# Two transformer layers and a mixture-of-experts block on one core: the first two halves of four projections multiplied tile by tile, with a new start and a new mixer order

## What is computed

```python
for l in range(DEPTH):                                   # DEPTH = 2, D_MODEL = 1024
    mod = silu_c @ w_mod[l] + b_mod[l]                   # shifts, scales and gates, six of each
    h = modulate(rms_norm(x, norm1[l]), sh1, sc1)        # and hc from ctx
    na_q, na_k, na_v, gq, gk, gv, ga, gb = split(h @ w_in[l])
    ...                                                  # two attentions
    x = x + g1 * branch_merge(ya, yb, ga, gb, w_pa[l], w_pb[l], w_o[l])
    h2 = modulate(rms_norm(x, norm2[l]), sh2, sc2)
    x = x + g2 * swiglu(h2, w_ffn_in[l], w_ffn_out[l])   # ctx too, in layer 0
x = rms_norm(x, final_norm)
# second block
conv_v, conv_g, lru_x, lru_g = split(rmsnorm(x, g_mix) @ w_in)
y_conv = silu(layernorm(causal_depthwise_conv(conv_v * sigmoid(conv_g), 31 taps)))
xr = causal_depthwise_conv(lru_x, 4 taps)
y_lru = rglru(xr) * gelu(lru_g)                          # gates from xr, a decay, a scan
x = x + concat(y_conv, y_lru) @ w_out
x = x + routed_experts(...); x = x + gate(x) * e
return rmsnorm(x, g_final)
```

## Time and profile before

| what | value |
|---|---|
| time, median of 3 runs | 3089.24 us (3089.12 to 3089.36) |
| the profiled execution's own time | 3086.72 us |
| its span, first to last instruction | 3084.8 us |
| TensorE busy | 2908.3 us, 94% of the span |
| VectorE, ScalarE, GpSimd busy | 958.2, 937.5, 829.0 us |
| mean granted TensorE clock | 0.975 |
| the start, to the first multiplication of x | 52.9 us |
| layer 0 / layer 1 | to about 1302 us / to about 2210 us |
| mixer | about 2210 to 2430 us |
| experts and output | from there |

### The profile page before, as it was taken

The page is one execution under the profiler, slowest core; times in us unless marked ns, Lnnn a source line. Parts: engine busy times, 40 slices in busy tenths (PEclk is TensorE's granted clock), DMA queues, the critical chain, the costliest instruction groups (busy, mean ns, idle before and its releaser), DMA issues.

```text
span 3084.8 us, 40562 instructions
## 1 busy us (share of the span) xinstructions
PE 2908.3 (94%) x16366; PEld 2149.8 (70%) x16366; DVE 958.2 (31%) x1409; ACT 937.5 (30%) x1598; POOL 829.0 (27%) x644
## 2 busy tenths in 40 slices
PE   6999889998999999999988989999989899999998
PEld 4887668887888888868767768888744744444443
DVE  2505550123111111160542122222487323232324
ACT  3226442123221122232643233222464211111131
POOL 3323223334222322443313444444410200000011
PEclk9999999999999999999999989999999899999999
DMA  5124321111111221212421222232220469999940
GB/s 206 55 69 165 110 90 62 61 62 48 62 59 57 69 68 51 79 41 79 155 83 63 88 96 82 84 110 88 87 87 28 198 287 402 409 401 409 401 194 27
DMA packets 62183, 406.48 MB, mean 132 GB/s; under 512 B 7232, under 2 KB 8656, under 8 KB 18160
## 3 DMA queue, kind: packets, MB, share of 16 engines
q1 hardware_dynamic: 57600, 393.77, 34.3%
q0 software_dynamic: 1872, 6.72, 0.6%
q10 hardware_dynamic: 2592, 4.30, 0.4%
HBM read 402.66 MB, written 2.10 MB: 131 GB/s over the span
## 4 chain that ended last, share of the span: by engine, by line
PE 79%; issue 8%; DVE 4%; ACT 4%; POOL 3%; DMA 1%; ACTq 0%; POOLq 0%; DVEq 0%
PE ps L585 45%; PE ps L1026 7%; PE ps L1049 4%; PE ps L753 3%; POOL half_slots L1619 3%; PE ps L780 3%; PE ps L734 3%; PE ps L1068 2%; PE ps L1096 2%; PE ps L992 2%; PE ps L621 2%; PE ps L594 1%; PE ps L913 1%; PE ps L610 1%; DVE expert_parts L2338 1%
## 5 line engine op out<-in xcount | busy, mean ns | idle before, releaser
L585 PE MATMUL ps<-h_parts,half_slots 128*128 128x512 f32 (+1 forms) x5952 | 1164.7, 357 | 38.1 <-POOL half_slots L1619 14.5
L585 PEld LDWEIGHTS ps<-h_parts,half_slots 128*128 128x128 f32 x5952 | 983.8, 190 | 219.0 <-issue 31.2
L1619 POOL TENSOR_TENSOR half_slots<-ring,half_slots 128x1024 fp32r<-128x1024 f32 (+3 forms) x280 | 600.1, 2144 | 1083.6 <-ACT half_slots L1164 1083.2
L1164 ACT ACTIVATE half_slots<-ring 128x1024 fp32r<-128x1024 f32 (+3 forms) x280 | 267.5, 956 | 1271.8 <-PE ps L585 1260.7
L585 PE MATMUL ps<-hidden_parts,half_slots 128*128 128x512 f32 (+1 forms) x1584 | 305.1, 355 | 0.0
L585 PEld LDWEIGHTS ps<-hidden_parts,half_slots 128*128 128x128 f32 x1584 | 261.0, 188 | 43.6
L585 PE MATMUL ps<-y_parts,half_slots 128*128 128x512 f32 (+1 forms) x1152 | 229.3, 359 | 9.9 <-DVE y_parts L1940 9.7
L1026 PE MATMUL ps<-second_block,scratch 128*64 128x512 f32 x1024 | 223.3, 594 | 1.4 <-ACT scratch L1549 0.9
L585 PEld LDWEIGHTS ps<-y_parts,half_slots 128*128 128x128 f32 x1152 | 192.9, 191 | 44.3 <-issue 11.8
L1026 PEld LDWEIGHTS ps<-second_block,scratch 128*64 128x64 f32 x1024 | 74.6, 137 | 142.8 <-issue 142.8
L1993 DVE TENSOR_TENSOR first_block<-ps,first_block 128x768 f32<-128x768 f32 (+1 forms) x44 | 36.3, 825 | 434.0 <-PE ps L585 434.0
(11 more groups left out here) (313 smaller groups left out, 2969.9 us busy)
## 6 DMA issues: line engine op xcount, KB each, us to landing
second_block<-experts SPq DMA_DIRECT2D x192, 1024.0 KB, 9.0
ring<-stream SPq DMA_DIRECT2D x146, 1024.0 KB, 4.8
ring<-stream SPq DMA_DIRECT2D x16, 768.0 KB, 4.2
...
```

What stands on the lines that cost most here:

```text
L585: last = nc.tensor.matmul(ps[s % 2][:, a:b], part(x, s)[:, k, :], parts[y][:, tile + k, a:b], start=start and k == 0 and n == 0, stop=stop ...
L1164: act.activation(part(0, s), raw_half(s), ACT.Copy).then_inc(hi_done, 1)
L1619: nc.gpsimd.tensor_tensor(part(1, s), raw_half(s), part(0, s).bitcast(fp32), ALU.subtract)\
```

## The change

1. *Start.* The eight `mod_head` slots get places of their own (`head_low`, `head_high`, in memory that is not yet used), so all eight transfers, one transfer for x behind the second of them, and the first slots of `gq` are issued at once. TensorE has the copied rows of two slots at a time (`HROW`), turns slot n-1 behind slot n's products, and sums squares and spreads 1/rms between slots (behind slots 4 and 6). The sums of squares are VectorE's, `rstd(0)` as well between its copies.
2. *First pair.* `first_pair` replaces the first two calls of `product` for `gq` and `ffn_in0` in both layers. The third half's parts go to a place outside `half_slots`, and `upper` for it waits one step less.
3. *Mixer.* TensorE: convolution, mean, gates, variance behind half 11. ScalarE and VectorE have the layer norm ahead of the recurrence; VectorE scales half 10 before its last five taps of tile 1. The sums lie in the free halves of banks 0 and 1.

```diff
+HEAD = 8
+def fills(n):
+    return 16 * ((n - HEAD) // RING + 1)
...
+        third = {}
+        for l in range(LAYERS):
+            third[2 * SLOT0[l, "gq"] + 2] = third_gq
+            third[2 * SLOT0[l, "ffn_in0"] + 2] = third_ffn
+
         def part(x, s):
+            if s in third:
+                return view(third[s], x * D, KD, P)
...
             def load(n, i=0):
                 m = n - RING
+                if m < HEAD:
+                    m = -1
...
+            for n in range(HEAD):
+                sp.dma_start(head_slot(n), stream[n]).then_inc(head_in[n // 2], 16)
+                if n == 1:
+                    sp.dma_start(X[:, :, :].rearrange("p k n -> p (k n)"), x_tiles).then_inc(x_loaded, 16)
...
+            def first_pair(s, nt, ready):
+
+                def tile(half, k):
+                    for a, b in pieces(nt):
+                        for n, (x, y) in enumerate(((0, 0), (0, 1), (1, 0))):
+                            last = nc.tensor.matmul(ps[half][:, a:b], part(x, s + half)[:, k, :], HS[y][:, k, a:b],
+                                                    start=k == 0 and n == 0, stop=k == KD - 1 and n == 2)
+                    if k == KD - 1:
+                        last.then_inc(steps, 1)
+
+                wait_half(s)
+                pe.wait_ge(lo_done, splits(s))
+                for k in range(KD + 1):
+                    if k < KD:
+                        ready(k)
+                        tile(0, k)
+                    if k == 1:
+                        wait_half(s + 1)
+                        pe.wait_ge(lo_done, splits(s + 1))
+                    if k:
+                        tile(1, k - 1)
...
-            for n in range(8):
-                mod_slot(n, 2 * n, 0, n == 0)
-            mod_turn()
+            for n in range(HEAD):
+                head_rows(n)
+                if n:
+                    head_turn(n - 1)
+                if n == 4:
+                    sum_squares(0, T)
+                if n == 6:
+                    spread_sum(0, T)
+            head_turn(HEAD - 1)
...
                 if j == 11:
-                    lru_gates()
                     convolve(0)
                     conv_mean()
-                if j == 12:
+                    lru_gates()
                     conv_variance()
...
-            for k in range(KD):
-                act.dma_start(X[:, k, 0:NL], xT[k * P:(k + 1) * P, :]).then_inc(x_loaded, 16)
-                act.dma_start(X[:, k, NL:T], ctxT[k * P:(k + 1) * P, :]).then_inc(x_loaded, 16)
...
-                act.wait_ge(steps, per * i + (s - 1))
+                act.wait_ge(steps, per * i + (s - 2 if s in third else s - 1))
...
+                root(2 * l, T)
                 if l == 0:
                     upper(2 * SLOT0[0, "gq"])
                     upper(2 * SLOT0[0, "gq"] + 1)
-                root(2 * l, T)
...
-            convolve(1, 20, TAPS)
+            convolve(1, 20, 26)
             scale_half(10)
+            convolve(1, 26, TAPS)
             scale_half(11)
             convolve(2, 2, TAPS)
```

161 lines of the change are left out of this document (107 added, 54 removed).

## The result

The changed kernel takes 3063.72 us (median; 3062.45 to 3065.93), the kernel before 3089.18 in the same comparison: a ratio of 0.9921, 95% interval 0.9909 to 0.9933, so 20.7 to 28.1 us less. Measured again later beside other variants it came out at 0.9931 (0.9917 to 0.9944). The forecast was 3068.8 us, 20.4 us less, inside 3060 to 3078. The two profiled executions of the changed kernel have spans of 3061.6 and 3066.3 us, against 3084.8.

The account below looks back on a forecast made before the run. TensorE, busy 94% of the span, was taken as the bound, with time to win only in its waits or half-clock matmuls. Terms 1.7 + 5.4 + 3.8 + 1.0 + 8.5 = 20.4 us gave 3068.8 us from 3089.24, range 3060 to 3078.

Parts of the forecast that it names:

- start: Program start: mod_head slots with own places and x as one transfer bring x's first multiplication to 51.2 us; gain 1.7 us.
- gq and ffn_in0, layer 0: Layer 0's first projection and FFN halves, alternated tile by tile: 2.7 us each (1.8 to 3.5), 5.4 us.
- gq, layer 1: Layer 1's first projection pair: h stays the bound, three tiles follow the last one in place of nine; gain 3.8 us.
- ffn_in0, layer 1: Layer 1's first FFN pair: S + 14.0 against S + 14.8; gain 1.0 us (0 to 2).
- mixer up to w_out2's third half: Second block's mixer, reordered: third half of w_out2 11.5 us earlier, less low-clock deductions; gain 8.5 us, ends 3 and 12.
- Rival 4: Start: x as one transfer needs 8 us at 386 GB/s or slows the kernel; 3089 to 3110, say 3098; chance 0.02.
- Rival 3: Pairs do nothing, alternating costs its gain or half 2 waits: 10 us fall away, 3079; chances 0.05, 0.03 with mixer eaten.
- Four gate products (1.7) run: Mixer, after the mean: four gate products take 1.7 us, then TensorE waits 2.3 us for ScalarE's squares and first sigmoid.
- the deduction for low clock: Mixer: about 1.5 us taken off behind the gates' wait, and 1.5 us behind the wait ahead of w_out2's third half.
- The tail keeps its order: Mixer after half 15: last lower part at 2376.5 (2388.0 before), w_out2's third half at 2386.3 instead of 2397.85.
- Rival 2: Mixer's gain eaten by low clock and ScalarE as bound for halves 14 and 15: 2 to 4 us remain, 3075; chance 0.17.
- Rival 1: Start reaches full clock: x multiplied at about 44 us, 7 us more gain, 3062; chance 0.16.

## Why the prediction was right, step by step

The forecast and its range held, and each term came near the trace, two of them in part by errors that cancelled (in us; the two traces of the changed kernel against the one of before):

| term | forecast | first | again |
|---|---|---|---|
| start | 1.7 | 2.4 | 1.9 |
| gq and ffn_in0, layer 0 | 5.4 | 5.3 | 4.9 |
| gq, layer 1 | 3.8 | 4.1 | 4.1 |
| ffn_in0, layer 1 | 1.0 | 1.8 | 0.6 |
| mixer up to w_out2's third half | 8.5 | 7.7 | 7.8 |
| sum | 20.4 | 21.3 | 19.3 |
| span | | 23.2 | 18.5 |

What lies between sum and span (+1.9 and -0.8) belongs to stretches that the change doesn't touch; it differs between traces of the same code, by 2 us in the attention, and by as much between w_out2 and the experts' first product.

*Start.* Right in its mechanism: slot 2 at 23.37 (forecast 23.6), then no gap, x at 50.49 and 50.98 (forecast 51.2). The number is near because two errors cancelled. From slot 2 to the last turn TensorE took 24.4 and 25.0 us instead of 26.9: a slot and its turn take 2.81 us from start to start, not 2.98, and the last turns ran at full clock. And what lies behind took 2.7 us instead of 0.7. x as one transfer cost nothing: it was there at 18.45 us, and from 10 to 22 us the changed kernel moved 429 GB/s where the earlier trace rows has 386. Rival 4 is out. That the splits of gq's weights, moved behind the last slot, would be ready in time held for TensorE (split by 52.6, first product at 54.1), but the move had a price that was not in it: it put GpSimd beside VectorE's gains, 2 us on the path to x. The forecast looked at when the result was needed, not at what ran beside it.

*Pairs.* Right: TensorE is the bound with 768 columns, in layer 1's gq h still is (its last lower part at 1322.1, the pair's end 2.4 us behind), no wait behind a pair, no loss from alternating banks. Of the 11.1 us, 8.0 are waits for GpSimd's parts; and the matmuls on h took 1161.9 us in all instead of 1164.7. Rival 3 is out. The spare place was rightly called the condition; without it 8.6 us of 11 were lost.

*Mixer.* That the reordering brings some 8 us is right, and shown by taking it back. That it came out at 7.7 against 8.5 is in part luck. The forecast's steps put the third half of w_out2 at 87.0 us behind half 11's end (98.5 less 11.5), and it then took 3 us off for low clock. The trace has it at 90.8, and the missing 3.8 us have other causes:

| us behind half 11's end | before | forecast | changed |
|---|---|---|---|
| half 15 done | 79.6 | 69.1 | 70.1 |
| from there to the last lower part | 9.2 | 8.1 | 10.9 |
| from there to the third half | 9.7 | 9.8 | 9.8 |

The first 1 us is the step "Four gate products (1.7) run", which is mis-sized: a product is two instructions of 0.45 us here, so four products take 3.60 [L998, x8]. The end of the variance is therefore 1.0 us later than forecast (42.1 against 41.1), the gates' wait was 0.47 us instead of 2.3, and the deduction for low clock behind it was not needed. The other 2.8 us are the step "The tail keeps its order". VectorE's instructions beside GpSimd's splits are stretched by some 3.9 us in all, before and now, but one that is stretched is now the gating (L2286). ScalarE waits for that before it copies half 15, which comes 4.1 us behind the half's end; before it was 2.0. The experiments above bear out both, the stretching and the order: with VectorE's own splits the 10.9 us are 8.2, with half 15 copied first 9.5, and with both 6.6. The wait of 3.9 us that the forecast has ahead of the third half was 0.53; 4.65 us stood ahead of the second four tiles. The clock behind that stayed at half until 2370.0, which cost TensorE 2.4 us in its matmuls, but none of it reached the third half: that is held by VectorE's eight multiplications and GpSimd's split, as before. Rival 2, ScalarE as the bound of halves 14 and 15, did not come: 64 matmuls in 28.00 us.

*Rival 1*, full clock in the start, did not come by itself in the stretch that the rival priced; only the last slot saw part of it (1.24 to 1.75 us in four of ten traces, 1.94 in the others). That activity alone releases the throttle, as the prediction sets beside this rival, is not borne out from 23.37 to 45.30: TensorE worked there without a gap and stayed at half clock. With full matmuls ahead it did come for slots 2 and 3, and the wait for the transfers kept it from deciding.
